# Rows 0 and 1 of the last product rounded inside the last pair's system, and five of its tiles placed between that system's steps

## What is computed

```python
def second_block(x, ...):
    h = rmsnorm(x, norm_gain)
    z = h @ w_in
    u_a, g_a, sh, g_b = parts of z
    y_a = multi_scale_pool(u_a, pool_w, pool_scale)          # 512 wide: 4 groups of 128
    y_b = rwkv7_time_mix(sh, ...)                            # 512 wide: 8 heads of 64
    y = concatenate([y_a * silu(g_a), y_b * silu(g_b)])      # 1024 wide
    x = x + y @ w_out
    return rmsnorm(x, final_gain)
```

## Time and profile before

| What | us |
|---|---|
| median of three runs | 1643.03 |
| the profiled execution, its own time | 1643.93 |
| its span, first to last instruction | 1642.1 |
| PE busy | 1572.7 (96%) |
| DVE busy | 784.8 (48%) |
| ACT busy | 617.2 (38%) |
| POOL busy | 525.8 (32%) |
| mean granted TensorE clock | 0.986 of full |

### The profile page before, as it was taken

The page is one execution under the profiler, slowest core; times in us unless marked ns, Lnnn a source line. Parts: engine busy times, 40 slices in busy tenths (PEclk is TensorE's granted clock), DMA queues, the critical chain, the costliest instruction groups (busy, mean ns, idle before and its releaser), DMA issues.

```text
span 1642.1 us, 31458 instructions
## 1 busy us (share of the span) xinstructions
PE 1572.7 (96%) x12684; PEld 1410.8 (86%) x12684; DVE 784.8 (48%) x1374; ACT 617.2 (38%) x1130; POOL 525.8 (32%) x233
## 2 busy tenths in 40 slices
PE   9999998999999999999999999999999989999895
PEld 8898978999999999999989788888889767778764
DVE  5444443744132231664447542322316798656645
ACT  4666674543232222432224532322224534433321
POOL 2222222044444444134440444444440244540020
PEclk9999999999999999999999999999999999999998
DMA  5111211122332222222322232232232122200001
GB/s 196 52 53 52 65 53 58 58 91 91 95 98 91 90 91 91 78 79 89 102 79 76 78 100 93 90 103 90 94 99 78 52 90 84 83 16 3 3 26 51
DMA packets 35690, 125.68 MB, mean 77 GB/s; under 512 B 4080, under 2 KB 4336, under 8 KB 35568
## 3 DMA queue, kind: packets, MB, share of 16 engines
q1 hardware_dynamic: 35568, 123.90, 23.3%
HBM read 121.79 MB, written 2.10 MB: 75 GB/s over the span
## 4 chain that ended last, share of the span: by engine, by line
PE 71%; DVE 10%; issue 3%; ACT 2%; DMA 0%; POOL 0%; DVEq 0%; ACTq 0%; SPq 0%; POOLq 0%
PE G L1435 59%; PE ST L1724 3%; PE G L1724 3%; PE ST L1407 2%; PE PV L1724 1%; PE PO L1724 1%; DVE rstd L874 1%; DVE wlo L913 1%; DVE t L1185 0%; DVE acc L1335 0%; DVE z L1188 0%; DVE m L933 0%; DVE z L1177 0%; ACT rms L542 0%; PE PO L1435 0%
## 5 line engine op out<-in xcount | busy, mean ns | idle before, releaser
L466 POOL TENSOR_TENSOR wlo<-raw,whi 128x1024 fp32r<-128x1024 f32 x207 | 502.5, 2429 | 1073.7 <-ACT whi L518 632.9
L1435 PE MATMUL G<-xh,whi 128*128 128x258 f32 (+3 forms) x1504 | 370.8, 309 | 11.4 <-DVE t L1019 6.9
L1435 PE MATMUL G<-xl,whi 128*128 128x258 f32 (+3 forms) x1504 | 358.3, 301 | 0.0
L1435 PE MATMUL G<-xh,wlo 128*128 128x258 f32 (+3 forms) x1504 | 356.7, 300 | 1.1 <-DVE xl L881 1.1
L1435 PE MATMUL G<-ah,whi 128*128 128x256 f32 (+2 forms) x1024 | 278.1, 312 | 4.7 <-DVE al L1160 2.9
L1435 PE MATMUL G<-al,whi 128*128 128x256 f32 (+2 forms) x1024 | 276.4, 311 | 0.0
L1435 PE MATMUL G<-ah,wlo 128*128 128x256 f32 (+2 forms) x1024 | 276.3, 311 | 0.0
L528 ACT ACTIVATE whi<-raw 128x1024 fp32r<-128x1024 f32 x112 | 118.7, 1060 | 419.1 <-PE G L1435 415.2
L1435 PEld LDWEIGHTS G<-xh,whi 128*128 128x128 f32 x1504 | 243.6, 189 | 30.2 <-issue 11.7
L1435 PEld LDWEIGHTS G<-xh,wlo 128*128 128x128 f32 x1504 | 244.7, 189 | 11.1 <-DVE xl L881 1.3
L1435 PEld LDWEIGHTS G<-xl,whi 128*128 128x128 f32 x1504 | 243.7, 189 | 10.6
(11 more groups left out here) (316 smaller groups left out, 2031.7 us busy)
## 6 DMA issues: line engine op xcount, KB each, us to landing
raw<-weights_dram SPq DMA_DIRECT2D x225, 512.0 KB, 3.5
hres<-xT_dram SPq DMA_DIRECT2D x8, 264.0 KB, 5.3
out_dram<-hres SPq DMA_DIRECT2D x8, 256.0 KB, 2.1
con<-consts_dram SPq DMA_DIRECT2D x1, 512.0 KB, 7.3
mat<-mats_dram SPq DMA_DIRECT2D x1, 512.0 KB, 8.0
con<-consts_dram SPq DMA_DIRECT2D x1, 264.0 KB, 6.6
vec<-vecs_dram SPq DMA_DIRECT2D x1, 171.0 KB, 6.5
con<-consts_dram SPq DMA_DIRECT2D x1, 128.0 KB, 4.4
```

The lines of the kernel that those rows point to most:

```text
L466: nc.gpsimd.tensor_tensor(wlo[:, s], raw[:, s % 2], whi[:, s].bitcast(F32), ALU.subtract)\
L1435: last_of[0] = nc.tensor.matmul(to[:, p0:p1], wt[:, w, ws], xt[:, k, t0 - off:t1_ - off], start=k == 0 and q == 0, stop=k == KT - 1 and q ...
```

## The change

It moves work and adds none. Three things change.

1. The order of tiles. `O2_TILES` now begins with rows 0 and 1 of all six blocks, then rows 2 to 5 block by block, then row 6 of all, then row 7.
2. Rows are split by steps of their own in the list (`row_`). Row 0 follows `td` half 0 of pair 3, row 1 follows `td` half 1, rows 2 and 3 open `ENDS`, and rows 4, 5 and 6 follow `norm` 4, 5 and 6 of pair 2.
3. Five tiles move into pair 3's system, behind `ht`, `z1`, `z2` and `z3` (second half each) and `q`. In `ENDS` one tile follows each of the first four steps (before: seven), two follow each later one.

PE's waits of the first tile change with it: the first tile waits for the copies of `w`, `bk` and `D8` of the last pair, whose banks it takes, and tile (4, 0) for those of `q` and `pt`.

```diff
 OPEN = 6
-O2_TILES = [(o, k) for o in range(OPEN) for k in range(KT - 1)] + [(o, KT - 1) for o in range(OPEN)]
+O2_TILES = [(o, k) for ks in ((0, 1), range(2, KT - 2)) for o in range(OPEN) for k in ks]
+O2_TILES += [(o, k) for k in (KT - 2, KT - 1) for o in range(OPEN)]
...
+        ROWS = {("td", 0): 0, ("td", 1): 1}
+        TILES = {("ht", 1): 0, ("z1", 1): 1, ("z2", 1): 2, ("z3", 1): 3, ("q", 0): 4}
...
+                    if p == PAIRS - 1 and t in ROWS:
+                        steps.append((row_, ROWS[t], "row", 0))
+                    if p == PAIRS - 1 and t in TILES:
+                        steps.append((out_, TILES[t], "out", 0))
...
-            ends, n = [], 0
+            ends, n = [(row_, 2, "row", 0), (row_, 3, "row", 0)], len(TILES)
             for i, t in enumerate(other):
                 ends.append(t)
-                more = min(n + (1 if i < KT - 1 else 2), O2_EARLY)
+                if t[1:3] == (PAIRS - 2, "norm"):
+                    ends.append((row_, t[3], "row", 0))
+                more = min(n + (1 if i < 4 else 2), O2_EARLY)
...
             for steps in (STEPS, ENDS):
-                if steps is ENDS:
-                    for k in range(KT - 1):
-                        last_high(k)
                 for kind, n, name, g in steps:
-                    if kind == system_:
+                    if kind == row_:
+                        last_high(n)
+                    elif kind == system_:
...
-                if steps is ENDS:
-                    last_low(0)
-                    last_low(1)
                 for kind, n, name, g in steps:
-                    if kind == system_:
+                    if kind == row_:
+                        last_low(n)
+                    elif kind == system_:
...
-                    elif kind == out_:
-                        if n + 2 < KT - 1:
-                            last_low(n + 2)
...
                 if (o, k) == (0, 0):
+                    pe.wait_ge(S("w_out"), PAIRS)
+                    pe.wait_ge(S("bk_out"), 2 * PAIRS)
+                    pe.wait_ge(S("d8_out"), 2 * PAIRS)
+                if (o, k) == (4, 0):
                     pe.wait_ge(S("q_out"), PAIRS)
                     pe.wait_ge(S("pt_out"), PAIRS)
```

More of the change, by code:

```diff
@@ L409, in woven @@
             return steps, ends + [(out_, j, "out", 0) for j in range(n, O2_EARLY)]
-        system_, tail_, mix_, out_ = range(4)
+        system_, tail_, mix_, out_, row_ = range(5)
         STEPS, ENDS = woven()
@@ L1364, in _ @@
                         tail(n, name, g)
-                    elif kind == out_:
-                        if n + 2 < KT - 1:
-                            last_low(n + 2)
-                    else:
+                    elif kind == mix_:
                         dve.wait_ge(S("mix_ready"), n + 1)
```

## The result

| | before | after |
|---|---|---|
| median, us | 1642.26 (1641.15 to 1643.71, 4 runs) | 1651.89 (1651.10 to 1652.48, 4 runs) |
| profiled execution, us | 1643.93 | 1652.43 |
| its span, us | 1642.1 | 1650.5 |
| mean granted clock | 0.986 | 0.984 |

(The median before now includes one run more than above.) The ratio is 1.0057, with a 95% interval of 1.0045 to 1.0069: the change makes the kernel slower. PE's busy time is 1574.6 us against 1572.7, so the loss is mostly waiting, not work.

What follows compares the result with a forecast made beforehand. Bound: the last pair's tail (its start, 14 half-steps, what follows `y`), not PE's tiles. 1.65 + 2.75 + 0.8 + 2.05 - 1.05 + 2.25 = 8.45 us on 1643.93 gives 1652.4, median 1651.5, range 1647.0 to 1654.0.

Steps and rivals of the forecast that it cites:

- Row 0 step: Row 0's low part on DVE, ahead of pair 2's chunk 6 UV, makes PE's `s` wait: +1.65 us.
- Five tiles: Five tiles between small matmuls of the last pair's system, 4.5 us less 1.75 covered by waits: +2.75 us.
- Start of the tail: Last pair's tail: DVE waits for row 6's high part before the copies for UV: +0.8 us.
- More tiles in the tail: Last pair's tail: all 14 half-steps have two tiles, where 3 had one: +2.05 us.
- the clock behind the wait: After PE's new 4.7 us wait before `s` of chunk 0, the clock drops: +2.25 us.
- Behind y: After `y`, ACT's last weight split no longer holds `sq`, and `var` follows sooner: -1.05 us.
- Behind row 7: After PE's start on row 7, clock already low before, so nothing added: between -1 and +0.7 us.
- POOL did not win: Rival: at the tail's start POOL gets ahead of DVE's copies, `s` waits 2.4 us more: 1653.9 us, 10%.
- The clock did not hold: Rival: the clock holds at the new wait before `s` of chunk 0, leaving 6.2 us: 1649.2 us, 17%.
- TensorE's work is not the bound: Rival: PE's queue, not the tail, sets the end, so removed waits are won: about 1640 us, 2%.

Runs made afterwards that it cites:

- no tiles in the joins: The changed kernel with the five tiles taken out of the last pair's system and put back in `ENDS`: 1651.2 us, ratio to before 1.0058.
- extra matmuls ahead of s: The changed kernel with 16 extra matmuls, results overwritten, in PE's 4.43 us wait before `s` of chunk 0: 1649.73 us, ratio to before 1.005.
- one tile to u of chunk 3: The changed kernel with one tile a step for the first seven steps of its last weave instead of four: 1652.95 us, ratio to before 1.0068.
- row steps behind the tail step: The changed kernel with the steps of rows 0 and 1 behind pair 2's tail step instead of ahead of it: 1650.59 us, ratio to before 1.0056.
- rows alone: The kernel before with only rows 0 and 1 moved under the last pair's system: 1643.52 us against 1643.18, ratio 1.0006.
- copies ahead of row 6: The changed kernel with row 6 split behind the first step of pair 3's tail instead of ahead of it: 1653.96 us, ratio to before 1.0074.
- tail-first order: The changed kernel's tile order, but the last pair's `u` and `s` right behind `pt`, norms and low parts between half-steps: 1636.47 us, ratio to before 0.9956.

## Why the prediction was right, and what was off in it

The forecast for the profiled execution was 1652.4 us, and it took 1652.43; the median of 1651.89 lies 0.4 us above the forecast 1651.5. That it came so near is luck in part. From T to row 7 the change cost 10.02 us where the sum has 8.45, and -1.38 us behind row 7 and -0.24 ahead of T, which the sum has at nothing, took that back.

- **Row 0 step:** forecast 1.65 us; 1.34 us in the raw start of `s` of chunk 6, 1.58 from T, 1.77 us at `pt` (no tiles in the joins, against before). Right in mechanism and size. What the prediction did not see is that by itself it is free at the chain's start. There the row steps took two low parts out of DVE's way, and the change put rows 5 and 6 in their place. The prediction counted "five low parts in both" and stopped there. Nor does it say that rows 2 and 3 now stand first: their high parts come only behind `pt` on ACT, and DVE waits 1.89 us for them, so that from there on all that delays `pt` delays the copies. By these rows it is this order that turns the 1.65 us into a loss; no run changes it alone.
- **Five tiles:** forecast 2.75, measured 3.39 us. The term was mis-sized by its unit. A tile among small matmuls costs 0.90 us from its start to that of the next group (1557.54 to 1558.44), but the small group ahead of it also takes 0.10 us longer (1556.93 to 1557.54, 0.61, where before it took 0.51; `q` 1.08 against 0.98). 5 x 1.00 - 3.39 leaves a cover of 1.6 us, where 1.75 was forecast.
- **Start of the tail:** forecast 0.8; `pt` to `s` went from 7.69 to 8.54 us, 0.85. The wait for row 6's high part has its row, and PE's idle time of 4.43 us was forecast as 4.7.
- **More tiles in the tail and the clock behind the wait:** forecast 2.05 + 2.25 = 4.3; `s` to `y` went from 25.45 to 30.12, 4.67 us. The clock alone is 2.6 us (extra matmuls ahead of s), so 2.1 us is left for the three tiles. The division was right. But taking the three tiles away won back only 0.95 us between `s` and `y`, in a profile in which the clock stayed low longer (one tile to u of chunk 3), and the clock's price behind the same wait was 1.5 us in another (29.03 against 27.53; row steps behind the tail step). So the 2.6 us belong to this execution, and that 2.25 was near them is luck in part.
- **Behind y:** forecast -1.05, measured 14.27 to 13.61 us, -0.66. ACT's split was out of `sq`'s way as expected, but `var` had three tiles ahead of it: 2.93 us behind `mu`.
- **Behind row 7:** forecast 0, with bounds of -1 and +0.7; measured -1.38 us, just outside. The clock was low before and after the start on row 7, but for a shorter time (4.48 us for the four tiles against 5.49). The longer wait is not the reason as far as the runs show. With the rows alone, where the wait is 3.07 us as before, this stretch is 32.30 us too, and in three other kernels with 7.89 us it is 33.16 to 33.56.

From T to row 7 that is +10.02 us (1.77 + 3.39 + 0.85 + 4.67 - 0.66). With -1.38 behind it and -0.24 ahead of T it gives the 8.4 us between the spans.

Of the rivals, POOL did not win, by 0.2 us, as forecast; that a loss would cost about what was said is shown by the copies ahead of row 6, which took 2.2 us more. The Trainium skill ("SBUF — State Buffer", section "Who interferes with whom") has the first to issue, of a DVE copy in a two-port mode and a POOL instruction, keep the port for its whole length. The runs agree: the first copy, which started 1.79 us behind POOL's instruction, was done only when that was. What happens where the starts are close is not settled by the rows: in the tail-first order DVE's norm step started 0.03 us ahead of POOL's split (1574.12 and 1574.15) and still took 2.96 us, POOL's its usual 2.38. The clock did not hold. TensorE's work is not the bound in this kernel; in the tail-first order it nearly is, with 5.0 us of waits left from 1560 us on.

## What to carry to other kernels

Filler work is worth placing only where the filled engine is the bound. Here PE waited for a serial chain, so every tile put ahead of a link of that chain was paid in full once its wait was used up. What paid was to start the chain at the first moment its input exists, and to spread the other engine's work between its links, where the tiles then cover it. When an instruction is taken out of an engine's queue, look at what takes its place there before the next critical one. And when a wait is removed, look at what it had held back on the other engines.

## What the runs showed of the hardware that was not expected

- The slow spell behind the last wait costs 1.4 to 2.8 us, and does not follow the wait's length. From row 7's first tile to the statistics of the output PE takes 16.87 us where the wait is filled (0.34 and 0.79 us left). It takes 19.69 us behind 3.07 us, but 18.25 behind the same wait with the rows alone. It takes 18.32 behind 7.89 us, but 19.18 to 19.60 in three other kernels with 7.89. Behind 1.01 and 2.02 us (tail first) it takes 16.88 and 16.87. So a wait of 2.02 us passed free here, one of 3.07 us in none of the profiles, and elsewhere in the kernel 1.72 us had brought the clock down: length alone does not decide it. What sets the length of the spell stays open.
- The same wait on the same code can cost or not. Ahead of `q` of pair 2, before anything that was edited, PE waits 1.72 or 1.73 us in all twelve profiles. In eleven the clock is down behind it and `q` takes 1.63 to 1.93 us; in the tail-first profile the granted clock stays at 1.00 and `q` takes 1.15 us. So a clock term of one profile should not be taken to a tenth of a microsecond.
- 12 matmuls whose result nobody reads, in a wait that was there anyway, make the kernel before 0.18% faster.
- DVE and POOL can each hold the other up. Two 64x64 copies under POOL's weight split took 2.60 us for 0.40, and the split took 4.12 us for 2.38 when three 128x512 instructions of DVE stood back to back over its start.
